# One wider matmul for the memory's two parts, and the last down products joined by transfers and read by 128-row tiles, in a one-core transformer layer

## The reference, cut to what matters

```python
def rms_norm(x, gain):
    y = xf * lax.rsqrt(jnp.mean(xf * xf, axis=-1, keepdims=True) + NORM_EPS)
    return y * gain

x = x + hybrid_mixer(rms_norm(x, ln_mix), ...)
m = rms_norm(mem, ln_mem)                  # mem: 256 tokens
k, v = jnp.split(m @ w_cross_kv, 2)        # w_cross_kv: 2048 x 4096
x = x + cross_attention(rms_norm(x, ln_cross), k, v, ...)
u = jax.nn.relu(rms_norm(x, ln_mlp) @ w_up)
x = x + (u * u) @ w_down                   # w_down: 8192 x 2048
return rms_norm(x, ln_final)
```

## Time and profile before

| what | value |
|---|---|
| median of 3 runs (lowest, highest) | 2839.78 us (2839.66, 2840.45) |
| the profiled execution's own time | 2841.27 us |
| its span in the trace | 2839.8 us |
| TensorE busy | 2801.2 us, 99% of the span |
| VectorE, ScalarE, GpSimd busy | 66%, 42%, 12% |
| memory windows in the trace | about 806 to 1007 us |
| last matmul starts | 2823.47 us |

### The profile page before, as it was taken

How to read it: one execution, slowest core, us unless ns; L and a number is a source line. 1 busy time by engine, 2 the same in 40 slices (tenths; PEclk the granted TensorE clock), 3 DMA queues, 4 the chain that set the end, 5 groups by cost and what they waited for, 6 DMA issues and landing times.

```text
span 2839.8 us, 42734 instructions
## 1 busy us (share of the span) xinstructions
PE 2801.2 (99%) x16624; PEld 2424.8 (85%) x16624; DVE 1884.5 (66%) x2073; ACT 1181.7 (42%) x1375; POOL 345.2 (12%) x400
## 2 busy tenths in 40 slices
PE   8999999999999999999999999999999999999997
PEld 5888777788889988889888899999998788888886
DVE  7545777755454443434445788888863888888888
ACT  5433433433454332423334365555553333333334
POOL 4000000000001123200111421212113100000001
PEclk9999999999999999999999999999999999999999
DMA  5333222232347874423333699999987756656555
GB/s 164 96 86 93 75 68 79 64 82 78 111 137 212 234 217 122 169 90 110 129 118 110 211 249 258 246 250 246 252 240 256 257 195 221 222 207 221 207 215 132
DMA packets 466144, 477.78 MB, mean 168 GB/s; under 512 B 10832, under 2 KB 369264, under 8 KB 465904
## 3 DMA queue, kind: packets, MB, share of 16 engines
q1 hardware_dynamic: 427136, 346.66, 39.9%
q0 software_dynamic: 38896, 129.56, 15.6%
HBM read 366.60 MB, written 81.79 MB: 158 GB/s over the span
## 4 chain that ended last, share of the span: by engine, by line
PE 91%; DVE 4%; DMA 2%; ACT 2%; issue 1%; POOL 0%; SPq 0%; DVEq 0%; ACTq 0%
PE slab_ps L1004 12%; PE slab_ps L1006 12%; PE slab_ps L1005 12%; PE down_ps L1651 7%; PE down_ps L1653 6%; PE down_ps L1652 6%; PE mix_ps L1594 6%; PE mix_ps L1593 6%; PE mix_ps L1595 6%; PE mix_ps L1006 2%; PE mix_ps L1005 2%; PE mix_ps L1004 2%; PE down_ps L1004 2%; PE down_ps L1006 2%; PE down_ps L1005 2%
## 5 line engine op out<-in xcount | busy, mean ns | idle before, releaser
L1004 PE MATMUL slab_ps<-act_hi,w_hi 128*128 128x512 f32 (+2 forms) x1928 | 721.4, 374 | 15.4 <-DVE act_lo L2421 10.6
L1006 PE MATMUL slab_ps<-act_hi,w_lo 128*128 128x512 f32 (+2 forms) x1928 | 698.5, 362 | 0.0
L1005 PE MATMUL slab_ps<-act_lo,w_hi 128*128 128x512 f32 (+2 forms) x1928 | 698.4, 362 | 0.0
L1679 ACT ACTIVATE w_hi<-w_raw 128x2048 fp32r<-128x2048 f32 x152 | 290.9, 1914 | 550.3 <-PE slab_ps L1006 414.9
L2369 DVE TENSOR_TENSOR w_lo<-w_raw,w_hi 128x2048 fp32r<-128x2048 f32 x152 | 349.4, 2298 | 233.4 <-ACT w_hi L1679 232.7
L1004 PEld LDWEIGHTS slab_ps<-act_hi,w_hi 128*128 128x128 f32 (+1 forms) x1928 | 364.0, 189 | 80.3 <-issue 23.7
L1006 PEld LDWEIGHTS slab_ps<-act_hi,w_lo 128*128 128x128 f32 (+1 forms) x1928 | 363.9, 189 | 57.9 <-issue 1.0
L1005 PEld LDWEIGHTS slab_ps<-act_lo,w_hi 128*128 128x128 f32 (+1 forms) x1928 | 364.4, 189 | 54.7 <-issue 5.3
L1651 PE MATMUL down_ps<-half_hi,u_slot 128*128 128x512 f32 x896 | 350.1, 391 | 2.6 <-DMA u_slot<-u_park 2.6
L1653 PE MATMUL down_ps<-half_lo,u_slot 128*128 128x512 f32 x896 | 349.9, 391 | 0.0
L1652 PE MATMUL down_ps<-half_hi,u_slot 128*128 128x512 f32 x896 | 349.8, 390 | 0.0
(11 more groups left out here) (484 smaller groups left out, 4889.7 us busy)
## 6 DMA issues: line engine op xcount, KB each, us to landing
b<-in_w_mlp_down_dram SPq DMA_DIRECT2D x64, 1024.0 KB, 6.7
w_raw<-in_w_in_dram SPq DMA_DIRECT2D x56, 1024.0 KB, 5.6
u_slot<-u_park SPq DMA_DIRECT2D x112, 512.0 KB, 8.4
w_raw<-in_w_mlp_up_dram SPq DMA_DIRECT2D x84, 512.0 KB, 7.8
w_raw<-in_w_cross_kv_dram SPq DMA_DIRECT2D x32, 1024.0 KB, 6.4
u_park<-u_hi POOLq DMA_DIRECT2D x32, 896.0 KB, 6.4
u_park<-u_lo POOLq DMA_DIRECT2D x32, 896.0 KB, 10.1
ucomb<-w_raw POOLq DMA_DIRECT2D x36, 512.0 KB, 7.9
```

The lines of the kernel that those rows point to most:

```text
L1004: mm(ps, wh, xh, start=first, stop=False)
L1005: mm(ps, wh, xl, start=False, stop=False)
L1006: return mm(ps, wl, xh, start=False, stop=last)
L1679: fn(w_hi[:, slot], w_raw[:, slot], ACT.Copy).then_inc(on["slab_hi"], 1)
```

## The change

`act_hi` and `act_lo` become the two halves of one tensor `act_both`. In a memory window, block k is now two matmuls: `w_hi` against both parts at once (2 times 256 columns into the two halves of the bank), and `w_lo` against the hi part into the first half. `kv_out` multiplies both halves of the bank by `mem_r` into two tiles of `msq` (128 by 512), waits for that, and adds them into `kv_t` (128 by 256).

In the down projection the last chunk stands outside of the loop and its last product is made tile after tile (`last_product`), each tile read by itself (`last_read`). All joins of n=0, and two of n=1 (B11 to B21, T2 to T3), are now nine pairs of transfers, spread from the third product of the last chunk on. ScalarE squares the n=0 tiles between weight halves 21 to 24, for which it waits at half 21 for fourteen join transfers. GpSimd multiplies the two n=0 tiles of tokens 0 to 255 by the gain, ScalarE scales them (`final_scaled`), and VectorE keeps six of the eight tiles. Only lines added and removed are shown:

```diff
@@ -208,8 +208,8 @@
-        act_hi = sb("act_hi", [P, KT, S], F32R)
-        act_lo = sb("act_lo", [P, KT, S], F32R)
+        act_both = sb("act_both", [P, 2, KT, S], F32R)
+        act_hi, act_lo = act_both[:, 0], act_both[:, 1]
@@ -419,9 +419,11 @@
+        gain_part = lambda n: b12[:, 2 * n:2 * n + 2].rearrange("p h (k d) -> p (h k) d", d=P)
-        FINAL_ORDER = [(2, 0), (3, 0), (2, 1), (3, 1), (0, 0), (1, 0), (0, 1), (1, 1)]
+        FINAL_ORDER = [(2, 0), (3, 0), (2, 1), (3, 1), (0, 1), (1, 1)]
+        SQUARES = 3 * NT
@@ -689,6 +691,8 @@
+                if n and t < 2:
+                    store(t, 0, "fin_squared", SQUARES + 1 + t)
@@ -975,23 +979,43 @@
-            first_cols = SLABS + 2 * PROD * NCH - PROD
+            done = SLABS + 2 * PROD * NCH
+            def products_read(n, q):
+                pool.wait_ge(on["slab_out"], done - PROD * (2 - n) + q + 1)
+            products_read(0, T2)
+            join(0, T2, B11)
+            products_read(0, B22)
+            join(0, B22, T1)
+            pool.wait_ge(on["cols0_joined"], 16 * 4)
+            join(0, B22, T2)
+            products_read(0, B21)
+            join(0, B21, B11)
+            products_read(0, T3)
+            join(0, T3, T2)
+            pool.wait_ge(on["cols0_joined"], 16 * 10)
+            products_read(0, T4)
+            join(0, T4, T3)
+            join(0, T1, T3)
+            pool.wait_ge(on["cols0_joined"], 16 * 14)
+            products_read(1, B11)
+            join(1, B21, B11)
-            pool.wait_ge(on["slab_out"], first_cols)
-            join(0, B22, T1)
-            join(0, B21, B11)
-            pool.wait_ge(on["fin_dve"], 1)
-            join(0, T3, T2)
-            pool.wait_ge(on["cols0_joined"], 16 * 6)
-            join(0, T4, T3)
-            join(0, T1, T3)
+            pool.wait_ge(on["cols0_joined"], 16 * 16)
+            products_read(1, T2)
+            join(1, T3, T2)
+            pool.wait_ge(on["fin_squared"], 4)
+            pool.wait_ge(on["vec_in"], 16 * 2)
+            for t in range(2):
+                nc.gpsimd.tensor_tensor(tile_part(t, 0), tile_part(t, 0), gain_part(0), ALU.mult).then_inc(
+                    on["acc_ready"], 1)
@@ -1004,6 +1028,11 @@
+            def memory_block(ps, wh, wl, k):
+                mm(ps, wh, act_both[:, :, k, 0:NMEM], start=k == 0, stop=False)
+                return mm(ps[:, 0], wl, act_hi[:, k, 0:NMEM], start=False, stop=k == KT - 1)
@@ -1021,8 +1050,11 @@
-                    last = hi_lo(G[slot][0:rows, 0:n], wh[:, k], wl[:, k], act_hi[:, k, 0:n], act_lo[:, k, 0:n],
-                                 k == 0, k == KT - 1)
+                    if n == NMEM:
+                        last = memory_block(halves(G[slot][:]), wh[:, k], wl[:, k], k)
+                    else:
+                        last = hi_lo(G[slot][0:rows, 0:n], wh[:, k], wl[:, k], act_hi[:, k, 0:n], act_lo[:, k, 0:n],
+                                     k == 0, k == KT - 1)
@@ -1653,10 +1685,33 @@
-            with pe.Fori(0, NCH) as c:
+            def last_product(c):
+                i = 2 * PROD - 1
+                bank = down_ps[(1, 0, 2, 3)[i % 4]]
+                pe.wait_ge(on["slab_out"], c * 14 + (SLABS + i - 3))
+                for t in range(2):
+                    for half in range(2):
+                        h = 2 * i + half
+                        if t == 0:
+                            pe.wait_ge(on["slab_lo"], c * 28 + (SLABS + h + 1))
+                        wh, wl = half_w[0][h % 4], half_w[1][h % 4]
+                        for j in range(2):
+                            uh, ul = (u_slot[T4][:, part, 2 * half + j, t * P:(t + 1) * P] for part in range(2))
+                            first, last = half == 0 and j == 0, half == 1 and j == 1
+                            mm(bank[:, t], uh, wh[:, j], start=first, stop=False)
+                            mm(bank[:, t], ul, wh[:, j], start=False, stop=False)
+                            ins = mm(bank[:, t], uh, wl[:, j], start=False, stop=last)
+                    ins.then_inc(on["slab_mul"], 1)
+            with pe.Fori(0, NCH - 1) as c:
+            for n in range(2):
+                for q in range(PROD - n):
+                    product(NCH - 1, n, q)
+            last_product(NCH - 1)
@@ -2311,15 +2366,21 @@
-            def final_rstd(a, done):
+            def final_rstd(tiles):
-                for t in (a, a + 1):
+                for t in tiles:
-                fn(fcols[:, 4, a:a + 2], fcols[:, 4, a:a + 2], ACT.Exp, scale=-0.5).then_inc(on["fin_rstd"], 1)
-                act.wait_ge(on["fin_rstd"], done)
+                both = slice(tiles[0], tiles[-1] + 1)
+                fn(fcols[:, 4, both], fcols[:, 4, both], ACT.Exp, scale=-0.5).then_inc(on["fin_rstd"], 1)
+            def final_scaled(t):
+                act.wait_ge(on["fin_rstd"], 2 + t)
+                act.wait_ge(on["acc_ready"], 3 + t)
+                fn(first(t), first(t), ACT.Copy, scale=fcols[:, 4, t:t + 1]).then_inc(on["fin_squared"], 1)
@@ -2331,26 +2392,29 @@
+                if h == 21:
+                    act.wait_ge(on["cols0_joined"], 16 * 14)
+                if 21 <= h < 21 + NT:
+                    t = (h - 19) % NT
+                    final_square(0, t, first(t))
+            half_hi(NCH - 1, 26)
-            act.wait_ge(on["fin_dve"], 5)
+            act.wait_ge(on["fin_dve"], 3)
-            half_hi(NCH - 1, 26)
-            act.wait_ge(on["cols0_joined"], 16 * 6)
-            act.wait_ge(on["fin_dve"], 7)
-            squares_of(0, 1, first)
-            final_rstd(2, 1)
-            act.wait_ge(on["fin_dve"], 8)
+            final_rstd((2, 3))
+            act.wait_ge(on["fin_dve"], 4)
-            act.wait_ge(on["cols0_joined"], 16 * 10)
-            squares_of(0, 0, first)
-            act.wait_ge(on["slab_out"], done)
-            squares_of(2, 0, left)
-            final_rstd(0, 2)
+            for t in range(2):
+                act.wait_ge(on["slab_out"], done + t)
+                final_square(2, t, left(t))
+                final_rstd((t,))
+            for t in range(2):
+                final_scaled(t)
@@ -2884,7 +2948,10 @@
-                tt(kv_t[:, slot], G[(slabs.first - 1) % 2][:, 0:NMEM], mem_r[:], ALU.mult).then_inc(on["slab_out"], 1)
+                parts = msq[:, 2 * slot:2 * slot + 2]
+                chain.link(tt(parts, halves(G[(slabs.first - 1) % 2][:]), mem_r[:].unsqueeze(1).broadcast_to([P, 2, NMEM]),
+                              ALU.mult))
+                tt(kv_t[:, slot], msq[:, 2 * slot], msq[:, 2 * slot + 1], ALU.add).then_inc(on["slab_out"], 1)
@@ -2905,11 +2972,13 @@
+                chain.count.enter(i - KV_SIDE // 2, 2)
+            chain.count.leave(KT - 1 - KV_SIDE // 2)
@@ -3297,15 +3366,14 @@
+                    elif q_ == B21:
+                        dve.wait_ge(on["cols0_joined"], 16 * 16)
+                    elif q_ == T3:
+                        dve.wait_ge(on["cols0_joined"], 16 * 18)
-                if last and q == 12:
-                    dve.wait_ge(on["slab_out"], done - PROD + 4)
-                    dve.wait_ge(on["fin_dve"], 1)
-                    dve.wait_ge(on["cols0_joined"], 16 * 6)
-                    join(0, B22, T2)
@@ -3330,25 +3398,25 @@
-            JOINED_BEFORE = {T2: 3, B22: 2, B21: 4, T3: 6, T4: 9}
+            JOINED_BEFORE = {T2: 2, B22: 1}
-                if i == 1:
-                    join(0, T2, B11)
-                elif i == 2:
+                if i == 2:
-                elif i == 3:
-                    join(1, B21, B11)
-                    dve.wait_ge(on["fin_dve"], 3)
+                    dve.wait_ge(on["fin_dve"], 2)
-                    join(1, T3, T2)
-                    dve.wait_ge(on["fin_dve"], 6)
+            def last_read(t):
+                bank = down_ps[(1, 0, 2, 3)[13 % 4]]
+                dve.wait_ge(on["slab_mul"], SLABS + 28 * NCH - 1 + t)
+                tt(acc[1][T4][:, t], acc[1][T4][:, t], blocks(bank)[:, t], ALU.add).then_inc(on["slab_out"], 1)
@@ -3372,17 +3440,17 @@
-                stt(out=tile_part(t, n), in0=tile_part(t, n), scalar=fcols[:, 4, t:t + 1],
-                    in1=b12[:, 2 * n:2 * n + 2].rearrange("p h (k d) -> p (h k) d", d=P), op0=ALU.mult,
+                stt(out=tile_part(t, n), in0=tile_part(t, n), scalar=fcols[:, 4, t:t + 1], in1=gain_part(n), op0=ALU.mult,
+            join(1, T4, T3)
+            dve.wait_ge(on["fin_dve"], 5)
+            last_read(0)
-                    join(1, T4, T3)
-                if place == 2:
-                    read(NCH - 1, 13, last=True)
-                final_tile(t, n, 1 if t >= 2 else 2)
+                    last_read(1)
+                final_tile(t, n, 1 if t >= 2 else 2 + t)
```

## The result

The changed kernel takes **2845.16 us** (median of 20 runs, 2842.36 to 2847.93); the kernel before takes 2839.87 us beside it (20 runs, 2838.47 to 2842.63). The ratio is **1.0018, 95% interval [1.0012, 1.0023]**. I had forecast 2836.0 with a range of 2832.7 to 2839.3: the forecast has the wrong sign, and the result lies outside of the range.

The account below looks back on a forecast made before the run. TensorE, busy 99% of the span, was taken as the bound, with full DMA engines a second bound in the tail. Gains of 2.3 + 1.5 = 3.8 us gave a median of 2836.0 us, range 2832.7 to 2839.3.

Parts of the forecast that it names:

- Two GpSimd multiplications: nothing: In the tail: two 128x1024 multiplications, 2.6 to 4.2 us each, start near 2812, wanted at 2826, so cost nothing.
- Nothing, with 2 us in hand: Last chunk: fourteenth join lands at about 2798 to 2802, so ScalarE's wait at half 21 costs nothing.
- limit at 2803.7: Last chunk: latest landing of the fourteenth join, since TensorE wants weight half 22 at 2807.4.
- rival 4: Last chunk: fourteenth join late, holding ScalarE and TensorE one for one past 2803.7; +10 us, 2846; 4%.
- the sum: Whole kernel: 2.3 us from the wide matmul plus 1.5 from the end, 3.8 us in all, giving 2836.0 us.
- The slower side: Whole kernel: slower by over 0.2%, from the late fourteenth join and unknowns, chance 0.05.
- Part A: Memory windows: wide matmul and longer eviction, 0.9 + 2.4 - 0.7 = 2.6 us, rounded down to 2.3.
- The heads: Mixer's heads, twice: windows 0 to 3 gain nothing, windows 4 and 5 gain 0.22 each; 0.9 us instead of 2.6.
- The loads: Memory windows 12 to 30: weight loads hold TensorE, leaving 2.4 us gain, or 4.2 if they never bind.
- The stage's end: After the last memory window: its 0.22 us gain lost and the eviction's extra 0.68 shown in full; -0.7 us.
- Part B: Down projection's end: VectorE ends 4.5 us earlier, stores take most of it back; 1.5 us gained.
- the gap over 0.5 us in the last chunk: Sign against the forecast: TensorE was to run without a gap from 2760 on.

Follow-up runs that it names:

- e4: Changed kernel with ScalarE's wait for the fourteen joins moved from half 21 to half 23, GpSimd's multiplications kept: 2839.42 us, ratio 0.9996 to the kernel before.
- e6: Changed kernel with GpSimd's two multiplications replaced by two fills of an unread buffer, gain left out of two output tiles: 2839.53 us, ratio 0.9997.
- e2: Kernel before with the down projection's new end alone, without the wide matmul: 2844.12 us, ratio 1.0016.
- e3: Changed kernel without GpSimd's multiplications and ScalarE's scalings; VectorE scales all eight tiles, wait stays at half 21: 2839.91 us, ratio 0.9999.
- e5: Changed kernel with VectorE scaling all eight tiles and ScalarE's wait for the joins two halves later: 2837.29 us, ratio 0.9990.
- e8: Kernel before with the wide matmul alone, loading only half of each memory-window weight: windows take 198.50 us against 201.40 with full loads.
- the mended kernels: Kernels with the new end, VectorE scaling all eight tiles and ScalarE's join wait two halves later: end 76.20 us with the wide matmul, 76.19 without.
- e12: Changed kernel with VectorE scaling all eight tiles, ScalarE's join wait two halves later and the last product computed and read whole: 2836.52 us, ratio 0.9990.

## Why the prediction was wrong, point by point

- **"Two GpSimd multiplications: nothing"** failed. Their length (2.87 and 3.35 us) was inside my 2.6 to 4.2. They started at 2814.6 in the time of the trace before, where I had 2812, and their results still came before they were wanted. I looked for who waits for their result, and not for what they do to the engine beside them. VectorE's addition at 2812.09 ends at 2815.52, 1.1 us behind the end of the first multiplication (2814.44); the one at 2815.45 ends at 2818.85, 1.1 behind the second (2817.76). Each waits for the multiplication to end, then runs. The row I had priced them from was itself a sign of it: the mean of 2.06 us for GpSimd's additions mixes 1.28 alone with 2.87 beside a split. That the length fell into my range was luck: begun beside no such VectorE instruction, a multiplication takes 2.40 us (e4), below the range. The Trainium skill has this on its page "SBUF — State Buffer" (section "SBUF: two separate sides"): VectorE with two SBUF inputs and a GpSimd instruction that reads SBUF exclude each other for a whole instruction. The trace agrees in each case that it shows: held with two SBUF inputs (3.43, 3.40, 2.49 us, and 1.71 instead of 0.68 in the kernel before), not held with one in PSUM (1.22, e4), not held by a fill (1.22, e6).
- **"Nothing, with 2 us in hand"**, for ScalarE's wait at half 21, failed by its landing. In the time of the trace before, the fourteenth join landed at 2805.05 (2762.16 plus the 42.89 us from the ninth split to ScalarE's 2802.01), 3 us beyond the 2802 I had given as the latest. The first group was the step that I had too short: its second pair waits for product B22, is issued 8.5 us behind the ninth split (2767.65 here), and its last transfer takes 10.7 us to land. The two groups behind it land 12.6 and 10.3 us after one another, where I had about 11. Timeline of the changed kernel, GpSimd:

```profile
2767.65 2.60 POOL L986 DMA_DIRECT2D main<-main  x2 [3.61 <-DVE main L3373]
...
2779.47 5.20 POOL L986 DMA_DIRECT2D main<-aside  x4 [9.22 <-DMA main<-main]
```

  The limit at 2803.7 was right, and so was rival 4's rule for TensorE, one for one: 1.35 us past it, TensorE lost 1.34; in e2, 0.4 past it, 0.38; in e3 and e6, just ahead of it, nothing there. What the rule lacks is the end. In e3 the last matmul is only 0.3 us late, but VectorE is late as well, the first store starts 1.43 us behind the last matmul instead of 0.61 (e5), and the end is 1.12 longer. So the wait had a price even at a landing inside the limit.
- **What the sum had no term for** is the meeting of the two. I priced each edit against the slack of the kernel before. ScalarE's wait used up VectorE's slack, and the multiplications would have needed the same slack. 2.5 (an estimate, at this landing) and 0.66 became 6.88, and 1.6 of that is the clock that fell behind the 3.3 us gap.
- **The slower side.** Rival 4 had the first of the two places, and 4%. It explains 1.3 of the 6.5 us by which the last matmul is late; that VectorE would be late, and then be held, stood in none of the rivals.
- **Part A** was nearly right. Block 0.347 us (measured 0.3467 or 0.3533), eviction 0.69 + 0.43 us (as priced), window distance 5.55 or 5.65. *The heads*: window 4 starts 29.70 us after the first cut (831.33), before at 29.7 (832.54); windows 0 to 3 gain nothing, as forecast. *The loads*: windows 15, 17 and 21 start 1.12, 0.70 and 0.11 us late, where I had 0.9, 0.65 and 0.7 (before, windows 15 and 17 were 0.43 and 0.20 late, where I had 0.5 together); with loads that never bind e8 gives 203.8 - 198.5 = 5.3 us, against my 0.9 + 4.2. *The stage's end*: from the last eviction to the end of the next split 10.6 us instead of 9.8, with 0.86 us between two starts on TensorE behind it: the -0.7 was right. I had +3.0 for the windows and -0.7 for their end; measured are +1.9 and -0.8. The slower pitch covers the difference: the changed kernel has it in 23 of its 32 windows, about 2.4 us, and e3, with little of it, gains 3.0. It stood in none of my rows, but the trace of before has a step of the same size in the down projection: in product B21 the matmuls are 0.233 us apart in every chunk, in its neighbours 0.2267.
- **Part B's gain** was right where it can be seen: 1.5 us forecast, and the mended kernels show 77.64 - 76.20 = 1.44. The stores take 14.3 us from the first one on in every version by tiles; before, 15.65. Only its cause was half right: without the product by tiles the new end gives 1.86, and the product by tiles, as read here, takes 0.4 back.
- Of the signs that I had named, the gap over 0.5 us in the last chunk is the one that came true against me.

By the traces the wide matmul is worth 1.9 - 0.8 = 1.1 us and the mended end 1.4 (1.9 with the last product whole). The medians of e5 and e12 lie 3.2 and 3.3 us below those of the kernel before beside them, where these sums say 2.5 and 3.0.

## What to carry to other kernels

Two edits that each hide behind the same engine's slack must be costed together: price the second one with the first one's delay in place. When work goes to GpSimd, ask what runs on VectorE at that moment and from where it reads, and look in the trace at hand for places where the two already run side by side: here a VectorE addition of 128x512 took 0.68 us alone and 1.71 beside a GpSimd multiplication; a reading GpSimd instruction can be put beside VectorE work that reads PSUM, or taken out. An early wait placed in front of an engine's regular work should be moved as late as its result allows, since here two halves later cost nothing, and joins that landed up to 2.2 us behind the old limit no longer held TensorE.

## What the runs showed of the hardware

- A VectorE addition with both inputs in SBUF that begins during a GpSimd multiplication takes 3.4 us instead of 1.22 (it ends 1.1 us behind the multiplication's end). A GpSimd fill of 2.7 us does nothing to it.
- It works the other way too. In the trace of before a GpSimd addition takes 1.28 us alone and 2.87 when it begins during a VectorE split with both inputs in SBUF, a GpSimd copy of 32 by 32 takes 2.27 us there, and a fill keeps its 0.55.
- Matmuls of 512 and 256 columns in turn have two pitches for the pair, 0.3467 and 0.3533 us, in one and the same execution; from window 12 on they change between them only where a window starts late. Three matmuls of 256 columns are 0.360 us. In the down projection the 512-column matmuls of product B21 are 0.233 us apart in every kernel, without a late start, and the others 0.2267.
- A TensorE gap of 3.3 us of idleness in the last chunk was followed by 3 us of matmuls 0.43 us apart; one of 1.86 us in the memory windows (e5) by a granted clock of 0.66 over 5 us. Idle gaps of up to 1.2 us (the changed kernel's first, 1.18; e12's at 906, 1.14) were followed by a granted clock of 1.00.
- Accumulating transfers on GpSimd's queue, issued in groups of four and six, each group waiting for the one before to land: the groups were issued 10 to 13 us after one another in the last chunk, and in nine executions the fourteenth landed 41.2 to 43.8 us behind the ninth split.
